# Four short TensorE transposes become plain fp32 matmuls, and the SBUF tiles are packed to 32 bytes instead of 64, in a two-layer hybrid encoder

## The chip, the cores and the metric

The kernel runs on one core of one Trainium2 chip. The metric is the device time of one execution in microseconds. Everything stays on one core, so there is no communication; the five engines (TensorE or PE, VectorE or DVE, ScalarE or ACT, GpSimd or POOL, and SyncE or SP, which only issues DMAs) work beside each other and meet through semaphores.

## The reference

Two layers over a sequence of 512 tokens of width 1024, in fp32. Each layer is

```
x = x + 0.5 * swiglu(rmsnorm(x, ffn1_norm), ...)          # D_FF = 2816
h = rmsnorm(x, mix_norm)
[q|k|v|g_out|a|b|glu|gates] = h @ w_in
q, k, v = silu(causal_conv4(q, k, v)); q, k = l2norm(q)/sqrt(128), l2norm(k)
beta = sigmoid(b);  g = -exp(a_log) * softplus(a + dt_bias)
o = gated_delta_chunked(q, k, v, g, beta)                 # 8 heads of 128
y_a = (rmsnorm(o, head_norm) * silu(g_out)) @ w_a_out
y_b = silu(rmsnorm(causal_conv31(val * sigmoid(gt)) + b, conv_norm)) @ w_b_out
x = x + (sigmoid(gate_a) * y_a + sigmoid(gate_b) * y_b) @ w_o
x = x + 0.5 * swiglu(rmsnorm(x, ffn2_norm), ...)
```

and a last `rmsnorm(x, final_norm)` follows. Inside the delta rule, with `gc` the cumulative sum of g within a chunk, the decays are `exp(gc_i - gc_j)`, a triangular system `(I + M) sol = rhs` is solved for each chunk, and the chunks of a head are then walked in order with a 128x128 state.

## The kernel before, in words

Activations lie transposed in SBUF: channels on the 128 partitions, the 512 tokens along the free axis, so a full tile is 128x512. The projections are "three-term" products: each fp32 weight tile is split into a rounded part `w_hi` and a rest `w_lo` in the fp32r format, the activations likewise (`h_hi`, `h_lo`, `act_hi`, `o_hi`, ...), and PE sums hi\*hi, hi\*lo and lo\*hi with 512 moving columns each (function `three`, line L414 for every matmul made through the helper `mm`). Weight tiles of 512 KB stream through four slots `raw`; ACT makes `w_hi`, and `w_lo` is made by DVE in the feed-forward parts and by ACT with an accumulating DMA from POOL in the mixer part.

The mixer part of a layer runs in nine sections, one PE instruction list (`PE_ORDER`) for each. In it the small fp32 products of one head's delta rule (a "round", eight per layer) are written by hand between the halves `H` of the projection of the next head, two three-term matmuls to an `H`:

```
PE_ORDER = "H H gr H H kt kk H kq H so H H x2t vt H H y0 fb H H xy0".split()
for _l in range(1, LEVELS):
    PE_ORDER += f"H H H H xt{_l - 1} y{_l} H H H xy{_l}".split()
```

PE follows this list in order, and each step waits for the semaphores of the step it needs. The steps the change touches:

- `gr` spreads the cumulative decay `gc` of the head over all partitions. It is four transposes (one for each 128-token chunk) of a single column of `hs`, read with stride 0 as a 128x128 matrix by `whole`. DVE reads the result in L1277 to form `dec`.
- `so` and `fb` belong to the head before (`tail`): `so` sums squares, DVE and POOL make the inverse root, and `fb` spreads it, again four transposes of a column. DVE uses it in L1348.
- `norm_spread` does the same for the inverse root of an RMSNorm: at the start of each feed-forward part, between the third and the fourth weight tile, and once before the mixer part of each layer.
- The last place is in the section after the ninth list, where the inverse root of the convolution's norm is spread into bank 6.

Other steps are transposes as well (`kt`, `x2t`, `vt`, `xt0` to `xt4` through the helper `turn`, L542; the entry transposes of x; the last ones of the output); these turn whole 128x128 tiles. Plain fp32 products of 128x128 tiles are made through `each`, for example `y0` to `y5` (NT with X) and `xy0` to `xy5`.

The feed-forward parts hold no such steps: PE runs through three-term products only, with DVE and ACT evicting.

All SBUF tiles are placed one behind another by the helper `sb`, each padded to a multiple of 64 bytes per partition; the counter is set back where tiles share space (`arena`, `dn_at`, `delta_at`).

Of the kernel before, what the change touches and what calls it, by code (L numbers as in the profile page):

```python
# [17 lines left out]
P = 128  # L18
# [34 lines left out]
HS_G, HS_GC, HS_NEG, HS_BETA, HS_KD, HS_GL, HS_N = 0, 1, 2, 3, 4, 5, 6  # L53
# [61 lines left out]
def trunk(nc, x, ffn1_norm, ffn1_w_gate, ffn1_w_up, ffn1_w_down, mix_norm, w_in, qkv_conv_w, a_log,  # L115
# [1 line left out]
          ffn2_w_gate, ffn2_w_up, ffn2_w_down, final_norm, consts, out):  # L117
    ds = bass.ds
    with ExitStack() as ctx:
        place = [(nc.sbuf_base + 63) // 64 * 64]  # L120

        def sb(name, shape, dt=F32):
            t = nc.alloc_sbuf_tensor_at(name, [P, *shape], dt, offset=place[0])
            place[0] += (4 * int(np.prod(shape)) + 63) // 64 * 64
            return t


        cst = sb("cst", [N_CONST, P])
        ident = cst[:, I_ID, :]
        incl = cst[:, I_INCL, :]  # L130
        ones = sb("ones", [P])
        xT = sb("xT", [KT, SEQ])
        h_hi = sb("h_hi", [KT, SEQ], F32R)
        h_lo = sb("h_lo", [KT, SEQ], F32R)
# [8 lines left out]
        nrm = sb("nrm", [4, NC])  # L143
# [37 lines left out]
        hs = sb("hs", [HS_N, NC])  # L181
        sm = sb("sm", [7, NC])
# [35 lines left out]
        bank = [ctx.enter_context(nc.psum_tensor(f"bank{i}", [P, SEQ], F32)) for i in range(8)]  # L218
# [96 lines left out]
        def whole(col):  # L315

            return col.broadcast_to([P, P])
# [94 lines left out]
        def _(pe):  # L412
            def mm(o, a, b, start=True, stop=True, **kw):
                return nc.tensor.matmul(o, a, b, start=start, stop=stop, **kw)  # L414
# [16 lines left out]
            def norm_spread(nf):  # L431
                pe.wait_ge(rs_done, nf + 1)
                for c in range(NC):
                    m = nc.tensor.transpose(bank[7][:, c * P:c * P + P], whole(nrm[:, 1, c:c + 1]), ident)
                m.then_inc(bc, 1)

            def ffn(l, w, r_f, v_f, r_d, v_d, nrm_i, nf, base_upd):
# [37 lines left out]
            for c in range(NC):  # L475
                pe.wait_ge(x_in[c], 16)
                for k in range(KT):
                    m = nc.tensor.transpose(bank[k][:, c * P:c * P + P], raw[c][:, k * P:k * P + P], ident)  # L478
                m.then_inc(xt_done, 1)

            with pe.Fori(0, DEPTH) as l:
# [3 lines left out]
                for k in range(KT):  # L485
                    m = nc.tensor.transpose(bank[k // 4][:, k % 4 * P:k % 4 * P + P], prow[:, k * P:k * P + P], ident)
# [7 lines left out]
                for k in range(KT):  # L494
                    pe.wait_ge((hlo_g, hlo_v)[k % 2], l * 4 + (k // 2 + 1))
                    for j, (wt, at) in enumerate(((wab_hi, h_hi), (wab_hi, h_lo), (wab_lo, h_hi))):
                        m = mm(bank[0][0:16, :], wt[:, k, :], at[:, k, :], start=(k == 0 and j == 0), stop=(k == KT - 1 and j == 2))
# [42 lines left out]
                def turn(o, a, name):  # L540
                    for c in range(NC):
                        m = nc.tensor.transpose(o[:, c * P:c * P + P], a[:, c * P:c * P + P], ident)  # L542
                    m.then_inc(*pe_dn.step(name))

                def stage(name, rn):

                    def ve(n, r=rn):
                        pe.wait_ge(ve_dn.sem, ve_dn.after(r, n))

                    def ac(n, r=rn):  # L550
                        pe.wait_ge(ac_dn.sem, ac_dn.after(r, n))

                    if name == "gr":
                        ve("hs")
                        for c in range(NC):
                            m = nc.tensor.transpose(bank[0][:, c * P:c * P + P], whole(hs[:, HS_GC, c:c + 1]), ident)
                        m.then_inc(*pe_dn.step(name))
                    elif name == "kt":
                        ve("kT")
                        turn(bank[1], kT, name)  # L560
                    elif name == "kk":
                        each(bank[2], kT, kT, name)
                    elif name == "kq":
                        ve("qT")
                        each(bank[3], kT, qT, name)
                    elif name == "vt":
                        ve("vT")
                        pe.wait_ge(ve_tl.sem, ve_tl.after(rn - 1, "og"))
                        turn(bank[4], va, name)
                    elif name == "x2t":  # L570
                        ve("x2T")
                        ac("eg")
                        turn(bank[0], XT, name)
                    elif name[0] == "y":
                        lv = int(name[1:])
                        ac("X2")
                        ac("kd")
                        if lv:
                            ve(f"x{lv - 1}")
                        each(bank[1], NT, X, name)  # L580
                    elif name[:2] == "xy":
                        pass
                    elif name[:2] == "xt":
                        ve("attnT")
                        ve(f"x{name[2:]}")
                        turn(bank[3], X, name)
                    elif name[:2] == "vn":
                        c = int(name[2:])
                        ac("vs")
                        if c:  # L590
                            ve(f"r{c}")
                        else:
                            ve(f"x{LEVELS - 1}")
                        mm(bank[1][:, 0:P], XT[:, c * P:c * P + P], (R[:, :] if c else vs[:, 0:P])).then_inc(*pe_dn.step(name))
                    elif name[:2] == "os":
                        c = int(name[2:])
                        t = slice(c * P, c * P + P)
                        ve(f"vn{c}")
                        pe.wait_ge(po_dn.sem, po_dn.after(rn, "qd"))
                        if c:  # L600
                            mm(bank[4][:, t], S[:, :], qd[:, t], stop=False)
                        m = mm(bank[4][:, t], VN[:, :], attn[:, t], start=(c == 0))
                        if c < NC - 1:
                            m = mm(bank[2][:, 0:P], kd[:, t], VN[:, :])
                        m.then_inc(*pe_dn.step(name))
                    elif name[0] == "p":
                        c = int(name[1:])
                        ve(f"s{c - 1}")
                        mm(bank[0][:, 0:P], kT[:, c * P:c * P + P], S[:, :]).then_inc(*pe_dn.step(name))

                def tail(name, rn):

                    if name == "so":
                        pe.wait_ge(po_tl.sem, po_tl.after(rn, "sum"))
                        pe.wait_ge(ve_tl.sem, ve_tl.after(rn - 1, "oF"))
                        for c in range(NC):
                            m = mm(bank[5][:, c:c + 1], attn[:, c * P:c * P + P], ones[:, 0:1])
                    else:
                        pe.wait_ge(po_tl.sem, po_tl.after(rn, "rs"))
                        for c in range(NC):  # L620
                            m = nc.tensor.transpose(bank[5][:, c * P:c * P + P], whole(sm[:, 5, c:c + 1]), ident)
                    m.then_inc(*pe_tl.step(name))

                def xy(lv, rn):
# [41 lines left out]
                for c in range(NC):  # L666
                    m = mm(bank[5][:, 8 + c:9 + c], csum[:, c * P:c * P + P], ones[:, 0:1])
# [9 lines left out]
                for m_ in range(PRE):  # L677
                    c = 2 * PRE + m_
                    first_unit(c)
                    for k in range(KT):  # L680
                        if m_ == 0 and k == 2:
                            pe.wait_ge(var_done, l * 4 + 3)
                            tail("so", last)
                        if m_ == 0 and k == 4:

                            pe.wait_ge(gate_done, l * (2 * PRE) + 5)
                            pe.wait_ge(rs_done, l * 4 + 3)
                            for q in range(NC):
                                m = nc.tensor.transpose(bank[6][:, q * P:q * P + P], whole(nrm[:, 1, q:q + 1]), ident)
                            m.then_inc(bc, 1)  # L690
                        if m_ == 0 and k == KT - 1:
                            tail("fb", last)
                            pe.wait_ge(ve_tl.sem, ve_tl.after(last, "olo"))
                        m = three(m_, c % SLOTS, k, o_hi, o_lo, k, k == 0, k == KT - 1)
                    m.then_inc(used, 1)
                for m_ in range(PRE):
                    c = 3 * PRE + m_
                    first_unit(c)
                    for k in range(KT):
                        if m_ == 0:  # L700
                            pe.wait_ge((clo_g, clo_v)[k % 2], l * 4 + (k // 2 + 1))
                        m = three(3 + m_, c % SLOTS, k, c_hi, c_lo, k, k == 0, k == KT - 1)
# [4 lines left out]
                with pe.Fori(0, N) as i:  # L707
                    for c in range(4):
# [7 lines left out]
                        for k in range(KT):  # L716
                            a_hi, a_lo = ((h_hi, h_lo), (h_hi, h_lo), (o_hi, o_lo), (c_hi, c_lo))[c]
                            m = three(c, c, k, a_hi, a_lo, k, k == 0, k == KT - 1)
                        m.then_inc(used, 1)

                with pe.Fori(0, 2) as i:
                    for j in range(4):
                        pe.wait_ge(lo_v, l * (V_LAYER * 4) + i * 4 + (V_O * 4 + j + 1 + SLOTS))
                        pe.wait_ge(x_upd, l * 24 + i * 4 + (16 + j - 1))
                        for k in range(KT):
                            if j == 0:
                                pe.wait_ge((mglo_g, mglo_v)[k % 2], l * 4 + (k // 2 + 1))
                            m = three(4 + j % 2, j, k, mg_hi, mg_lo, k, k == 0, k == KT - 1)
# [5 lines left out]
            for c in range(NC):  # L734
                for half in range(2):
# [3 lines left out]
                    for k in range(4):  # L739
                        m = nc.tensor.transpose(bank[n % 2][:, k * P:k * P + P], xT[:, 4 * half + k, c * P:c * P + P], ident)  # L740
# [870 lines left out]
```

## Time and profile before

| | |
|---|---|
| Runs | 2936.02, 2940.02, 2941.77 us; median 2940.02 us |
| Profiled execution | 2941.77 us, its span 2939.9 us |
| Busy share of the span | PE 97%, PE weight loads 80%, DVE 55%, ACT 38%, POOL 11% |
| Mean granted TensorE clock | 0.984 |
| DMA | 297.11 MB, mean 101 GB/s |

The span runs from the first to the last instruction of the profiled execution; 1.9 us lie around it. Times in the profile are in microseconds from the start of the span unless marked ns. "PE" is the matmul stream and "PEld" the weight loads that overlap it; the end of a matmul is modelled, so starts are the surer reading. A granted clock of 1.00 is 2.4 GHz and 0.50 is 1.2 GHz; a stretch with a change in it shows a value between. In the groups by line, the names behind `bank<-` are the operands.

### The profile page before, as it was taken

How to read it: one execution, taken by the hardware profiler on the slowest of the kernel's cores; microseconds unless marked ns; L12 is line 12 of the kernel's file. 1: busy time of each engine (PE TensorE's matmuls, PEld its weight loads, DVE VectorE, ACT ScalarE, POOL GpSimd, SP SyncE). 2: the span in 40 equal slices, each digit the busy share in tenths (PEclk: the TensorE clock that was granted, in tenths of full speed). 3: DMA queues.
4: the chain of work that ended last, by engine and by line, in shares of the span. 5: the costliest groups of instructions: out<-in, count | busy, mean ns of one | idle time of the engine just before them, and what ended most of it. 6: DMA issues, size and time to landing. Idle time of an engine off the chain costs nothing.

```text
span 2939.9 us, 40643 instructions
## 1 busy us (share of the span) xinstructions
PE 2841.8 (97%) x13920; PEld 2365.8 (80%) x13920; DVE 1623.9 (55%) x2435; ACT 1111.0 (38%) x1647; POOL 334.8 (11%) x292
## 2 busy tenths in 40 slices
PE   7999988999999999999999999799999999999999
PEld 6888867888887888888878888588888878788887
DVE  5554235888887355553255542378888853554532
ACT  4222244555553233332233222455555532323321
POOL 1000021211222010000000000221122210200001
PEclk9999989999999999999999999899999999999999
DMA  4333268666663433333333333797676745333332
GB/s 141 99 100 93 79 115 106 117 117 107 116 118 85 98 93 93 94 98 92 91 94 100 93 97 77 132 88 128 118 106 110 117 87 98 93 93 99 91 98 68
DMA packets 479234, 297.11 MB, mean 101 GB/s; under 512 B 12181, under 2 KB 462869, under 8 KB 479093
## 3 DMA queue, kind: packets, MB, share of 16 engines
q1 hardware_dynamic: 462964, 236.63, 36.6%
q0 software_dynamic: 16128, 58.73, 10.4%
q8 instruction: 72, 1.18, 0.2%
q14 instruction: 70, 0.57, 0.1%
HBM read 234.51 MB, written 2.10 MB: 80 GB/s over the span
## 4 chain that ended last, share of the span: by engine, by line
PE 84%; DMA 5%; DVE 4%; ACT 4%; issue 3%; POOL 0%; ACTq 0%; DVEq 0%; POOLq 0%; SPq 0%
PE bank L414 81%; DMA raw<-in_w_in 3%; DMA w_lo<-raw 2%; PE bank L542 2%; ACT w_hi L751 1%; ACT w_lo L753 1%; DVE cacc L1176 0%; DVE NT L1295 0%; ACT NT L886 0%; DVE XT L1300 0%; DVE w_lo L1004 0%; ACT thv L882 0%; PE bank L478 0%; DMA raw<-in_ffn_w_gate 0%; ACT dec L889 0%
## 5 line engine op out<-in xcount | busy, mean ns | idle before, releaser
L414 PE MATMUL bank<-h_hi,w_hi 128*128 128x512 f32 x2432 | 968.4, 398 | 22.9 <-DVE h_lo L1031 13.9
L414 PE MATMUL bank<-h_lo,w_hi 128*128 128x512 f32 x2432 | 969.8, 399 | 0.0
L414 PE MATMUL bank<-h_hi,w_lo 128*128 128x512 f32 x2432 | 968.2, 398 | 0.0
L751 ACT ACTIVATE w_hi<-raw 128x1024 fp32r<-128x1024 f32 x448 | 472.0, 1057 | 649.7 <-PE bank L414 604.9
L1004 DVE TENSOR_TENSOR w_lo<-raw,w_hi 128x1024 fp32r<-128x1024 f32 x336 | 413.5, 1232 | 537.9 <-ACT w_hi L751 537.0
L414 PEld LDWEIGHTS bank<-h_hi,w_hi 128*128 128x128 f32 x2432 | 461.2, 190 | 112.2 <-DVE h_lo L1031 15.4
L414 PEld LDWEIGHTS bank<-h_lo,w_hi 128*128 128x128 f32 x2432 | 461.9, 190 | 86.6
L414 PEld LDWEIGHTS bank<-h_hi,w_lo 128*128 128x128 f32 x2432 | 461.1, 190 | 85.4
L1176 DVE SCALAR_TENSOR_TENSOR cacc<-c_raw,ncol,cacc 128x512 f32<-128x512 f32 x464 | 380.7, 821 | 9.3
L414 PE MATMUL bank<-act_hi,w_hi 128*128 128x512 f32 x704 | 273.9, 389 | 0.0
L414 PE MATMUL bank<-act_lo,w_hi 128*128 128x512 f32 x704 | 273.9, 389 | 0.0
L414 PE MATMUL bank<-act_hi,w_lo 128*128 128x512 f32 x704 | 273.9, 389 | 0.0
L778 ACT ACTIVATE hf<-hf 128x512 f32<-128x512 f32 x88 | 55.6, 632 | 439.6 <-DVE hf L1046 439.6
L1495 POOL TENSOR_TENSOR ssq<-ssq,sqb 128x512 f32<-128x512 f32 x42 | 54.1, 1287 | 1440.7 <-ACT sqb L761 1440.7
L1487 POOL DMA_DIRECT2D w_lo<-raw x112 | 97.8, 907 | 595.5 <-ACT w_lo L753 575.0
L414 PEld LDWEIGHTS bank<-act_hi,w_hi 128*128 128x128 f32 x704 | 132.1, 188 | 27.7
L414 PEld LDWEIGHTS bank<-act_lo,w_hi 128*128 128x128 f32 x704 | 132.1, 188 | 27.3
L414 PEld LDWEIGHTS bank<-act_hi,w_lo 128*128 128x128 f32 x704 | 132.1, 188 | 27.3
L1048 DVE TENSOR_TENSOR sqb<-bank,ssq 128x512 f32<-128x512 f32 x88 | 60.8, 691 | 132.9 <-PE bank L414 132.7
L753 ACT ACTIVATE w_lo<-raw 128x1024 fp32r<-128x1024 f32 x112 | 118.8, 1060 | 0.0
L1046 DVE TENSOR_TENSOR hf<-bank,ssq 128x512 f32<-128x512 f32 x88 | 60.8, 691 | 102.8 <-PE bank L414 102.6
L874 ACT ACTIVATE XT<-bank 128x512 f32<-128x512 f32 x80 | 48.3, 604 | 150.9 <-PE bank L542 150.9
(238 smaller groups left out, 3127.3 us busy)
## 6 DMA issues: line engine op xcount, KB each, us to landing
raw<-in_w_in SPq DMA_DIRECT2D x128, 512.0 KB, 9.0
w_lo<-raw POOLq DMA_DIRECT2D x112, 512.0 KB, 7.3
raw<-in_ffn_w_gate SPq DMA_DIRECT2D x88, 512.0 KB, 3.8
raw<-in_ffn_w_up SPq DMA_DIRECT2D x88, 512.0 KB, 3.8
raw<-in_ffn_w_down SPq DMA_DIRECT2D x64, 512.0 KB, 3.6
raw<-in_ffn_w_down SPq DMA_DIRECT2D x32, 384.0 KB, 3.2
raw<-in_w_a_out SPq DMA_DIRECT2D x16, 512.0 KB, 4.3
raw<-in_w_b_out SPq DMA_DIRECT2D x16, 512.0 KB, 3.6
```

The source lines that it names most:

```text
L414: return nc.tensor.matmul(o, a, b, start=start, stop=stop, **kw)
L542: m = nc.tensor.transpose(o[:, c * P:c * P + P], a[:, c * P:c * P + P], ident)
L751: nc.scalar.activation(w_hi[c % SLOTS][:, :], raw[c % SLOTS][:, :], ACT.Copy).then_inc(hi_done, 1)
L753: nc.scalar.activation(w_lo[c % SLOTS][:, :], raw[c % SLOTS][:, :], ACT.Copy, scale=-1.0).then_inc(neg_done, 1)
L778: nc.scalar.activation(sg_f[c // 2][:, :], sg_f[c // 2][:, :], ACT.Silu).then_inc(silu_done, 1)
L874: nc.scalar.activation(XT[:, :], bank[3][:, :], ACT.Copy).then_inc(*ac_dn.step(f"XT{lv - 1}"))
L1004: tt(w_lo[c % SLOTS][:, :], raw[c % SLOTS][:, :], w_hi[c % SLOTS][:, :].bitcast(F32), ALU.subtract).then_inc(lo_v, 1)
L1046: tt(sg_f[f][:, :], bank[c][:, :], ssq[:, :], ALU.mult).then_inc(gs_done, 1)
L1048: tt(a_f[f][:, :], bank[c][:, :], ssq[:, :], ALU.mult).then_inc(ub_done, 1)
L1176: stt(out=dst, in0=src, scalar=ncol[:, j:j + 1], in1=cacc[:, :], op0=ALU.mult, op1=ALU.add).then_inc(taps, 1)
L1487: pool.dma_start(out=w_lo[c % SLOTS][:, :].bitcast(F32), in_=raw[c % SLOTS][:, :], accum_op=ALU.add).then_inc(lo_g[c % SLOTS], 16)
L1495: tt(ssq[:, :], ssq[:, :], sqb[m % 2][:, :], ALU.add).then_inc(sums, 1)
```

## The change

Four places that call the transpose instruction of TensorE with the identity as moving operand now call the plain matmul with the same two operands. In `gr` the operands change too: the column is `g` itself instead of its cumulative sum, and the moving matrix is the triangular matrix of ones `incl` instead of the identity, so that the product forms the cumulative sum. The waits and the other engines' instructions stay. And `sb` pads to 32 bytes instead of 64.

```diff
-        place = [(nc.sbuf_base + 63) // 64 * 64]
+        place = [(nc.sbuf_base + 31) // 32 * 32]
 
         def sb(name, shape, dt=F32):
             t = nc.alloc_sbuf_tensor_at(name, [P, *shape], dt, offset=place[0])
-            place[0] += (4 * int(np.prod(shape)) + 63) // 64 * 64
+            place[0] += (4 * int(np.prod(shape)) + 31) // 32 * 32
             return t
...
             def norm_spread(nf):
                 pe.wait_ge(rs_done, nf + 1)
                 for c in range(NC):
-                    m = nc.tensor.transpose(bank[7][:, c * P:c * P + P], whole(nrm[:, 1, c:c + 1]), ident)
+                    m = mm(bank[7][:, c * P:c * P + P], whole(nrm[:, 1, c:c + 1]), ident)
...
                     if name == "gr":
                         ve("hs")
                         for c in range(NC):
-                            m = nc.tensor.transpose(bank[0][:, c * P:c * P + P], whole(hs[:, HS_GC, c:c + 1]), ident)
+                            m = mm(bank[0][:, c * P:c * P + P], whole(hs[:, HS_G, c:c + 1]), incl)
...
                         pe.wait_ge(po_tl.sem, po_tl.after(rn, "rs"))
                         for c in range(NC):
-                            m = nc.tensor.transpose(bank[5][:, c * P:c * P + P], whole(sm[:, 5, c:c + 1]), ident)
+                            m = mm(bank[5][:, c * P:c * P + P], whole(sm[:, 5, c:c + 1]), ident)
...
                             for q in range(NC):
-                                m = nc.tensor.transpose(bank[6][:, q * P:q * P + P], whole(nrm[:, 1, q:q + 1]), ident)
+                                m = mm(bank[6][:, q * P:q * P + P], whole(nrm[:, 1, q:q + 1]), ident)
```

## Rows read from the trace of the kernel before

**Rows 1.** The page: busy time of the engines, and the chain that ended last.

```profile
PE 2841.8 (97%) x13920; PEld 2365.8 (80%) x13920; DVE 1623.9 (55%) x2435; ACT 1111.0 (38%) x1647; POOL 334.8 (11%) x292
...
PE 84%; DMA 5%; DVE 4%; ACT 4%; issue 3%; POOL 0%; ACTq 0%; DVEq 0%; POOLq 0%; SPq 0%
```

**Rows 2.** Groups on PE, shapes apart: count, then busy us, mean ns, idle before.

```profile
L414 PE MATMUL bank<-X,NT 128*128 128x128 f32 x768 | 102.5, 277 | 0.0
...
L556 PE MATMUL bank<-cst,hs 128*128 128x128 f32 x64 | 10.9, 297 | 9.3 <-DVE hs L1267 9.3
...
L621 PE MATMUL bank<-cst,sm 128*128 128x128 f32 x64 | 9.6, 272 | 0.0
...
L434 PE MATMUL bank<-cst,nrm 128*128 128x128 f32 x24 | 4.6, 326 | 6.1 <-POOL nrm L1499 6.1
```

**Rows 3.** Timeline of PE in a round: start us, us, instruction, count.

```profile
703.92 0.60 PE L542 MATMUL bank<-cst,X 128*128 128x128 f32 x4
704.35 1.06 PE L414 MATMUL bank<-X,NT 128*128 128x128 f32 x8
705.16 0.48 PE L414 MATMUL bank<-h_lo,w_hi 128*128 128x512 f32 x1
705.48 0.39 PE L414 MATMUL bank<-h_hi,w_lo 128*128 128x512 f32 x1
705.71 0.40 PE L414 MATMUL bank<-h_hi,w_hi 128*128 128x512 f32 x1
```

**Rows 4.** Timeline of PE at the start of the first feed-forward part.

```profile
43.86 0.60 PE L434 MATMUL bank<-cst,nrm 128*128 128x128 f32 x4
...
44.53 0.39 PE L414 MATMUL bank<-h_lo,w_hi 128*128 128x512 f32 x1
```

**Rows 5.** Timeline of the start of a steady round; in brackets idle before, and releaser.

```profile
627.39 0.60 PE L556 MATMUL bank<-cst,hs 128*128 128x128 f32 x4
...
628.02 1.13 DVE L1277 TENSOR_SCALAR dec<-bank,hs 128x128 f32<-128x128 f32 x4
...
631.37 0.17 DVE L1283 TENSOR_SCALAR sm<-ksum 128x4 f32<-128x4 f32 x1 [0.96 <-ACT NT L886]
...
633.49 0.40 PE L414 MATMUL bank<-h_hi,w_hi 128*128 128x512 f32 x1
...
634.59 0.65 PE L542 MATMUL bank<-cst,XT 128*128 128x128 f32 x4 [0.70 <-DVE XT L1300]
```

**Rows 6.** Chain that ended last, same round: start us, us, what.

```profile
611.82 14.37 PE bank L414 x76
...
626.29 0.05 ACT hf L849
...
637.70 0.44 PE bank L621 x4
```

**Rows 7.** Waits of PE, whole span: total us, times, longest.

```profile
PE bank L542 <- DVE XT L1300: 10.7, 14, 1.1
...
PE bank L414 <- DMA w_lo<-raw: 8.5, 3, 3.1
```

**Rows 8.** Busy time by stretch: the columns end with granted clock, DMA share, GB/s.

```profile
512.70:516.20 3.50, 3.44 (x10) 2.84 (x11) 0.54 (x3) 2.96 (x4) 0.00 (x0) 0.52 0.80 129
```

**Rows 9.** Chain that ended last, before and in the first round of layer 0.

```profile
394.99 1.13 PE bank L434 x4
...
451.20 0.95 PE bank L556 x4
```

**Rows 10.** Chain that ended last, last round of layer 0 and the section after.

```profile
896.37 0.73 DVE XT L1261
...
918.35 0.44 PE bank L689 x4
...
920.87 0.45 PE bank L621 x4
```

**Rows 11.** One line of DVE: duration ns min/median/max.

```profile
L1176 DVE SCALAR_TENSOR_TENSOR cacc<-c_raw,ncol,cacc x464: 726/752/2097, 470.5 to 2358.6; 128x512 f32<-128x512 f32 x155
```

## The prediction

> **What bounds the kernel now.** I read the page first: PE is busy 97% of the span, and the chain of work that ended last runs over PE for 84% of it [rows 1]. So what PE must do longer is paid unless it falls into one of PE's few waits. Next I read the groups of PE with the shapes kept apart, to see what a transpose and a plain fp32 product of the same size are on this engine [rows 2]; then the timeline of PE, for what each costs in the stream [rows 3, 4]; then the timeline and the chain of one steady round, the waits of PE, and the places outside the steady rounds, to see which of the changed steps has a wait behind it that swallows it [rows 5 to 10].
>
> The reader is to see two things. First, the code asks for 4 x 6 x 16 = 384 products `NT,X`, and the trace has 768 matmuls of that form; for `gr` it asks for 4 x 16 = 64 transposes, and the trace has 64 [rows 2]. A plain fp32 product is two weight loads with two matmuls, a transpose is one. Second, in a round PE waits in one place, for DVE L1300 before `x2t`, about 0.7 us [rows 5]; in all 14 such waits with 10.7 us [rows 7], in 14 of the 16 rounds.
>
> **The cost of one group of four.** The step of the stream is 0.23 us for a three-term matmul [rows 3]. From the start of four transposes to the second matmul behind them are 44.53 - 43.86 = 0.67 us [rows 4]; less one step of 0.23, four transposes take 0.44. From the start of four transposes, with eight plain matmuls (four products) behind them, to the second matmul behind those are 705.48 - 703.92 = 1.56 us [rows 3]; less 0.23 and 0.44, four plain products take 0.89. So each group that changes costs PE 0.89 - 0.44 = 0.45 us more at full clock. At the low clock, the same columns take twice the time: a group of four at 394.99 stands with 1.13 us where it has 0.60 at full clock [rows 4, 9], so I take 0.9 us there.
>
> The Trainium skill, TensorE: Matmul & The Clock Gate, section Terms, calls the transpose mode four times faster for FP32. By that a plain group would take 1.76 us instead of 0.89 and the change would cost 1.32 a group instead of 0.45. The trace does not agree: it shows 0.89 for four products, twice the transposes, and I go by the trace.
>
> **The change part by part.** The groups: `gr` 64/4 = 16, `fb` 64/4 = 16, `norm_spread` 24/4 = 6 [rows 2], and two in bank 6 (one per layer): 40.
>
> - *`fb`, 12 in the rounds.* It stands between `y0` and the halves that follow, behind the wait at `x2t`, and it is on the chain (L621 at 637.70) [rows 6]. Nothing waits between it and the end of the round; the next round's wait does not shrink either, since the work that it waits for starts with ACT L849 at 626.29, right behind PE's last three-term matmuls of the section before [rows 6]: it moves with PE. 12 x 0.45 = 5.4 us. The rounds are 16; the first of each layer has no `fb` before it, and the last of each layer ends otherwise (next).
> - *`fb`, 2 in the last round of each layer.* That round has all 31 taps of the convolution on DVE, and the chain goes over DVE before the first `vn` (XT L1261 at 896.37) [rows 10]. PE is ahead of DVE there: 0. Without that cover, 0.9.
> - *`fb` for the last head, 2, and bank 6, 2.* Both are on the chain at 918.35 and 920.87, with DVE waiting [rows 10]: 4 x 0.45 = 1.8.
> - *`norm_spread` in the feed-forward parts, 4.* PE runs without a break there [rows 4]: 4 x 0.45 = 1.8.
> - *`norm_spread` ahead of the mixer part, 2.* On the chain, at the low clock [rows 9]: 2 x 0.9 = 1.8.
> - *`gr`, 12 in rounds with the wait.* PE reaches `x2t` 0.45 later and finds it not later: its last matmul before starts at 633.49, so it could go on at 633.72, and XT comes at 634.59; 0.87 us of slack for 0.45. But `gr` also feeds DVE: L1277 would start at 628.47 instead of 628.02 and DVE be 0.45 later until L1283, where it sits idle 0.96 us for ACT's squares [rows 5]. Both covers are wider than the delay: 0. What is late next without them is `x2t` itself, 0.45 each.
> - *`gr`, 2 in the first round of each layer.* PE starts it out of a wait for `hs`, at the low clock, and everything of the round hangs on it (L556 at 451.20 is on the chain) [rows 9]: 2 x 0.9 = 1.8. In layer 0 one of the three waits for the `w_lo` transfer [rows 7] comes before the next round and may swallow it.
> - *`gr`, 2 in the rounds without the wait at `x2t`.* These are the second rounds; that of layer 0 is at the low clock (granted 0.52 from 512.7) [rows 8]. 0.9 + 0.45 = 1.35.
> - *`incl` for the identity, `g` for `gc`.* Same shape, another 128x128 tile of the same constant array; 0. `gc` is still made, since DVE needs it.
> - *32 bytes instead of 64.* Tiles from `hf` on move down by 32 to 256 bytes. Some, among them `act_hi`, `o_hi`, `c_hi` and `mg_hi`, come to lie at 32 bytes past a multiple of 64. No big DMA target moves. DVE's taps read `c_raw` at every multiple of 4 bytes, and of 464 the shortest takes 726 and the median 752 ns [rows 11] (the longest are held up by something else), so the start address makes no difference above some 3% on DVE. PE's moving operand at such an address is in no row. I take 0; the bound above is in the rivals.
>
> Sum: 5.4 + 1.8 + 1.8 + 1.8 + 1.8 + 1.35 = 13.95, so 14 us. Against the profiled execution, 2941.77 us, that is 2955.8; it lies 1.75 us above the median of the runs, 2940.02, so the forecast for a median is 2954 us, slower by 0.48%.
>
> **The rivals.**
>
> - *All 40 groups are paid.* Something in the 12 rounds moves with `gr` after all, say ACT's squares behind `kt`, which is also 0.45 later. Then 12 + 2 more groups: 14 x 0.45 = 6.3, in sum 20.3 us: 2960. Against it are the 0.96 us of idle DVE and 0.87 us of PE [rows 5]; for it, that the chain to `x2t` runs through ACT right behind. 12 in 100.
> - *Not slower: a round's pace is not PE's.* If DVE or the weight transfers set when a round ends, whatever PE gets in one vanishes; it decides from the point where they need 0.45 us more than PE in each round. Left are 8 groups outside the rounds at full clock and the two ahead of the mixer parts at the low one: 8 x 0.45 + 2 x 0.9 = 5.4 us: 2945.4, +0.18%. For it are three waits for a transfer with 8.5 us; against it, that they are three in the whole span [rows 7] and that the steady round's chain is PE's [rows 6]. 10 in 100.
> - *The address costs on PE.* If a moving row off a multiple of 64 bytes cost one cycle of 2.4 GHz for each 64 bytes, that would be 32 cycles, 13 ns, for each of 3264 matmuls over `act`, `o`, `c` and `mg` (by the code's loops 2112 + 3 x 384): 43 us more, 2997 in all. No row speaks for it; the nearest, DVE's taps, speaks against. 5 in 100.
> - *The plain product costs more than in `each`* (four times a transpose): the 20 open groups at 1.32, 26; the low clock ones at 2.6, 14; `gr` past its slack of 0.87 twelve times, 5: 45 us, 2985. 2 in 100.
> - *Faster through the clock.* The granted clock is 0.984 in the mean; if plain matmuls in place of transposes brought it up sooner after each of PE's waits, the gain would be half of the low stretch they cut. To end faster by 0.2% it would have to give 20 us, cutting 40 us of low clock. The stretches at the low clock next to changed groups are about 3 to 4 us each [rows 8] and six in number, 24 us in all. 2 in 100.
>
> The Trainium skill (same page, Part 4: PE-mode transpose) says that transposes do not count as busy for the clock. If so, the first rounds' `gr` and the two spreads would bring the clock up to 0.9 us sooner, worth up to 0.45 each, and the sum would be 12 instead of 14.
>
> **How the numbers follow.** A measurement of this kernel tells about 0.2%, 5.9 us, from no change (its three runs lie within 5.75 us). The forecast's own chance is 66 in 100, with 3 left for what I have not seen. The range goes from the rival with 5.4 us, 2945, to a little past the rival with all groups paid, 2962; it leaves out the address, the dear product and the faster clock. Slower by over 0.2%: 87 in 100; within 0.2%: 11; faster: 2.
>
> **What would show it.** In the profile after, the forms at `gr`, `fb` and the spreads should be counted twice, 128 for each 64, and PE have 160 more matmuls. From `y0` to the second matmul behind `fb` should be 0.45 us more. The wait at `x2t` should shrink from 0.7 to about 0.3 us, with `x2t` no later behind ACT L849. The step of the stream should stay 0.23 us over `act_hi` as over `h_hi`. I am wrong if rounds keep their length, if `x2t` moves with `gr`, or if that step changes.

## The result and the profile after

The changed kernel takes 2970.5 us in the median of four runs (2968.7 to 2972.0), the kernel before 2940.9 in four runs on the same chip (2936.0 to 2945.4). The medians lie 29.6 us apart. The ratio is 1.0095, 95% interval 1.0082 to 1.0108, which is 28 us; the record holds ten runs of the changed kernel in all, from 2965.5 to 2972.0, with a mean of 2968.7. So it is slower by 28 us, where 14 were forecast and 2962 was the upper end of the range.

The page after, first the busy time of each engine and then the chain that ended last:

```profile
PE 2879.1 (97%) x14080; PEld 2388.2 (80%) x14080; DVE 1622.7 (55%) x2435; ACT 1110.2 (37%) x1647; POOL 334.9 (11%) x292
...
PE 87%; DVE 4%; ACT 3%; DMA 3%; issue 3%; POOL 0%; ACTq 0%; DVEq 0%; POOLq 0%; SPq 0%
```

PE has 160 matmuls more, as foreseen, and still bounds the kernel; its share of the chain rose [rows 1]. The groups of PE after, shapes apart (count, busy us, mean ns of one, idle before):

```profile
L414 PE MATMUL bank<-h_lo,w_hi 128*128 128x512 f32 x2432 | 968.0, 398 | 0.0
...
L414 PE MATMUL bank<-act_hi,w_hi 128*128 128x512 f32 x704 | 279.1, 396 | 0.0
L414 PE MATMUL bank<-act_lo,w_hi 128*128 128x512 f32 x704 | 279.1, 396 | 0.0
L414 PE MATMUL bank<-act_hi,w_lo 128*128 128x512 f32 x704 | 279.1, 396 | 0.0
L414 PE MATMUL bank<-X,NT 128*128 128x128 f32 x768 | 102.2, 276 | 0.0
...
L414 PE MATMUL bank<-cst,hs 128*128 128x128 f32 x128 | 18.9, 295 | 11.1 <-DVE hs L1267 11.1
L414 PE MATMUL bank<-cst,sm 128*128 128x128 f32 x128 | 16.9, 275 | 0.0
L414 PE MATMUL bank<-cst,nrm 128*128 128x128 f32 x64 | 10.5, 316 | 5.5 <-POOL nrm L1499 5.5
```

The forms of `gr` and `fb` stand twice as often as before [rows 2]. The other thing to see is the products over `act`, which no edit to a matmul touched. In the kernel before they and those over `h` stood so:

```profile
L414 PE MATMUL bank<-h_lo,w_hi 128*128 128x512 f32 x2432 | 969.8, 399 | 0.0
...
L414 PE MATMUL bank<-act_hi,w_hi 128*128 128x512 f32 x704 | 273.9, 389 | 0.0
```

Over `act` they are no longer at 389 ns but at 396, while over `h` hardly anything moved. Matmuls overlap, so their mean duration isn't what the stream pays; that is the distance from one start to the next. The timeline of PE after, in the down projection of the first feed-forward part:

```profile
299.94 0.40 PE L414 MATMUL bank<-act_hi,w_hi 128*128 128x512 f32 x1
300.18 0.39 PE L414 MATMUL bank<-act_lo,w_hi 128*128 128x512 f32 x1
300.41 0.40 PE L414 MATMUL bank<-act_hi,w_lo 128*128 128x512 f32 x1
300.64 0.40 PE L414 MATMUL bank<-act_hi,w_hi 128*128 128x512 f32 x1
300.88 0.39 PE L414 MATMUL bank<-act_lo,w_hi 128*128 128x512 f32 x1
```

and in the same projection of the kernel before:

```profile
298.65 0.39 PE L414 MATMUL bank<-act_hi,w_hi 128*128 128x512 f32 x1
...
299.56 0.39 PE L414 MATMUL bank<-act_lo,w_hi 128*128 128x512 f32 x1
```

Four steps take 0.94 us after, 0.235 each, and 0.91 before. Rounded to 0.01 us that is hardly to be told from 0.23, so from here on I give the *step*: the mean distance of successive starts in the trace over all three-term matmuls of one operand that follow each other within 260 ns. Over `act` it went from 226.7 to 234.3 ns, over `o` from 227.3 to 234.0, over `mg` from 226.9 to 234.2; over `h` (227.8 and 227.5) and `c` (231.7 and 231.3) it stayed. Times their counts, 2112 x 7.6 = 16.1 us for `act` and 768 x 7.1 = 5.4 us for `o` and `mg`: 21.5 us that the sum of the forecast had at 0.

The same, by stretches of the two profiled executions (spans 2939.9 and 2967.5 us, so +27.6). The marks are POOL L1499, which ends each norm's inverse root, and DVE L1267, which starts each round:

| stretch | change, us |
|---|---|
| four feed-forward parts, from one L1499 to the next | +4.44, +4.42, +4.44, +4.44 |
| rounds 3 to 8 of each layer (5 distances of L1267) | +1.82, +1.98 |
| from the inverse root to the third round | +2.77, -1.03 |
| eighth round to the inverse root behind it | -0.27, -0.23 |
| output projections and `norm` up to the feed-forward part | +1.40, +4.48 |
| start and end of the kernel | -0.19, -0.91 |

Each feed-forward part holds 528 matmuls over `act` (4.0 us) and one group of `norm_spread` (0.45). Together that is 4.45 us, where 4.42 to 4.44 were measured.

The steady round after, in the timeline of its engines (in brackets the idle time before, and its releaser):

```profile
633.66 0.60 ACT L849 ACTIVATE hf<-bank 128x512 f32<-128x512 f32 x1 [3.11 <-PE bank L414]
...
634.76 1.05 PE L414 MATMUL bank<-cst,hs 128*128 128x128 f32 x8
...
635.85 1.13 DVE L1277 TENSOR_SCALAR dec<-bank,hs 128x128 f32<-128x128 f32 x4 [0.50 <-PE bank L414]
...
638.73 0.17 DVE L1283 TENSOR_SCALAR sm<-ksum 128x4 f32<-128x4 f32 x1 [0.50 <-ACT NT L886]
...
641.96 0.65 PE L542 MATMUL bank<-cst,XT 128*128 128x128 f32 x4 [0.24 <-DVE XT L1300]
...
644.91 1.06 PE L414 MATMUL bank<-cst,sm 128*128 128x128 f32 x8
645.72 0.47 PE L414 MATMUL bank<-h_hi,w_lo 128*128 128x512 f32 x1
646.03 0.39 PE L414 MATMUL bank<-h_hi,w_hi 128*128 128x512 f32 x1
```

Against [rows 5, 6]: from ACT L849 to `x2t` are 8.30 us before (626.29 to 634.59) and 8.30 after (633.66 to 641.96). The idle time ahead of `x2t` went from 0.70 to 0.24 us, that ahead of DVE L1283 from 0.96 to 0.50. From the start of `fb` to the second matmul behind it are 1.12 us, 0.89 without one step.

### The profile page after: what moved, and what is told of

It reads as the page before. It is cut to its first block, busy times and chain, and to the rows that moved or that the text cites. A ratio compares the mean times of both kernels' runs of the same rounds, so it can differ in the third digit from the quotient of the medians.

```text
span 2967.5 us, 40963 instructions
## 1 busy us (share of the span) xinstructions
PE 2879.1 (97%) x14080; PEld 2388.2 (80%) x14080; DVE 1622.7 (55%) x2435; ACT 1110.2 (37%) x1647; POOL 334.9 (11%) x292
## 4 chain that ended last, share of the span: by engine, by line
PE 87%; DVE 4%; ACT 3%; DMA 3%; issue 3%; POOL 0%; ACTq 0%; DVEq 0%; POOLq 0%; SPq 0%
PE bank L414 85%; PE bank L542 2%; DMA raw<-in_w_in 2%; ACT w_hi L751 1%; DMA w_lo<-raw 1%; ACT w_lo L753 1%; ACT NT L886 1%; DVE NT L1295 1%; DVE cacc L1176 0%; DVE XT L1300 0%; ACT dec L889 0%; ACT qd L890 0%; PE bank L478 0%; DVE w_lo L1004 0%; DMA raw<-in_ffn_w_gate 0%
```

## The experiments

Two parts are to be told apart, the matmuls and the padding. Of the second, I wanted to know what about the addresses matters.

**`e1_pad32`**: the padding alone.

```diff
-        place = [(nc.sbuf_base + 63) // 64 * 64]
+        place = [(nc.sbuf_base + 31) // 32 * 32]
...
-            place[0] += (4 * int(np.prod(shape)) + 63) // 64 * 64
+            place[0] += (4 * int(np.prod(shape)) + 31) // 32 * 32
```

> The kernel before with the 32-byte padding alone; all transposes stay. Theory A (the address of PE's moving operand costs): the step of the three-term stream is 234 ns over act, o and mg, as in the changed kernel, where it is 227 before, and 228 over h; with 7.4 ns for 2112 matmuls over act and 7 for 768 over o and mg this gives 21 us, 2961 us. Rival B (the slower step comes with the plain matmuls, not with the addresses): step 227 everywhere, 2940 us.

**`e2_matmuls`**: the four edits to the matmuls alone, padding as before.

> The four matmul edits alone, padding 64 bytes as before. Theory A: step 227 ns over act; the time is the sum of the prediction for the matmuls, or somewhat less, since six of the steady rounds of layer 0 and 1 are only 0.4 us longer each: 7 to 14 us, 2947 to 2954 us. Rival B: step 234 ns over act, about 2965 us or more.

Times against the kernel before on the same chip (2938.1 us, 27 runs): the padding alone 2954.8 (6 runs), ratio 1.0057 [1.0033, 1.0082]; the matmuls alone 2948.5 (10 runs), 1.0038 [1.0024, 1.0052]. Together 0.95%, the whole. The same group on PE in the first and then in the second:

```profile
L414 PE MATMUL bank<-act_hi,w_hi 128*128 128x512 f32 x704 | 279.1, 396 | 0.0
```

```profile
L414 PE MATMUL bank<-act_hi,w_hi 128*128 128x512 f32 x704 | 273.9, 389 | 0.0
```

The steps of the first are those of the changed kernel (`act` 234.3, `o` 234.0, `mg` 234.3), those of the second those of before (226.7, 227.0, 226.9). The steps make 21.5 us. The median of the padding alone grew by 16.7 us, with 10 to 24 by the interval. The span of its profiled execution grew by 21.8, but that execution is the slowest of its six (2963.6 us), so the close match with 21.5 is partly luck. The rounds of the first take 56.37 us as before (56.40), those of the second 56.87.

**`e3_gr`** and **`e4_fb`**: one line each.

```diff
-                            m = nc.tensor.transpose(bank[0][:, c * P:c * P + P], whole(hs[:, HS_GC, c:c + 1]), ident)
+                            m = mm(bank[0][:, c * P:c * P + P], whole(hs[:, HS_G, c:c + 1]), incl)
```

> Only gr as plain matmuls, padding 64 bytes. If gr is hidden behind the wait before x2t, a steady round stays 56.40 us from hs to hs and the wait of PE shrinks from 0.70 to about 0.3 us; in all 0 to 3 us more, 2940 to 2943 us. Rival: each round 0.45 us longer, 7 us in all, 2947 us.

```diff
-                            m = nc.tensor.transpose(bank[5][:, c * P:c * P + P], whole(sm[:, 5, c:c + 1]), ident)
+                            m = mm(bank[5][:, c * P:c * P + P], whole(sm[:, 5, c:c + 1]), ident)
```

> Only fb as plain matmuls, padding 64 bytes. If fb is paid in each steady round, that round is 56.8 to 56.9 us from hs to hs instead of 56.40, and the whole 6 to 7 us longer, 2947 us. Rival (something else sets the pace of a round): a round stays 56.40 us and the time 2941 us or less.

`gr` alone: 2938.0 us (10 runs), 0.999 [0.9974, 1.0007], steady rounds of 56.40 to 56.43. For all of `gr` this interval ends at 2 us more. `fb` alone: 2942.8 (10 runs), 1.0024 [1.001, 1.0039], which is 7 us [3, 11], though the medians lie only 4.7 apart; its steady rounds take 56.86, which is 0.46 more. The steady round of `gr` alone, timeline:

```profile
629.84 0.60 ACT L849 ACTIVATE hf<-bank 128x512 f32<-128x512 f32 x1 [3.17 <-PE bank L414]
...
630.93 1.05 PE L414 MATMUL bank<-cst,hs 128*128 128x128 f32 x8
...
638.14 0.65 PE L542 MATMUL bank<-cst,XT 128*128 128x128 f32 x4 [0.25 <-DVE XT L1300]
```

Again 8.30 us from L849 to `x2t`; the whole of the longer `gr` went into the wait, 0.70 to 0.25. `fb` has no such wait behind it in a steady round and is paid. What the edits do outside the steady rounds can't be told from single profiles: from the inverse root to the third round of a layer, the two layers of before take 176.2 and 175.1 us, those of `gr` alone 179.4 and 174.5, those of `fb` alone 171.7 and 171.7, those of all four edits 180.4 and 176.7. They differ by more than the 4.95 us that the forecast put there, and `fb` alone is shorter than before.

**`e5_arena32`, `e6_arena64`, `e7_arena96`**: the kernel before, with a gap of 32, 64 or 96 bytes ahead of `arena`. `act`, `o`, `mg` and all behind them move up by so much; the weight slots and `h` stay.

```diff
+        place[0] += 32
         arena = place[0]
```

> The kernel before with 32 bytes left free ahead of the arena, so that every tile from x_sq on starts 32 bytes higher and nothing else moves against anything. If the start of PE's moving operand past a multiple of 64 bytes is the cause: step 234 ns over act, o and mg, 227 over h, about 21 us more. If another of the moved tiles of the change was the cause (hf, small ones): step 227.

> As the run with 32 bytes, but with 64, which puts the arena's tiles at 64 past a multiple of 128 and c_lo, which was at 64 before, at a multiple of 128. If only the distance from a multiple of 64 bytes counts: step 227 ns over act, o and mg, the time as before. If the distance from a multiple of 128 counts: 234 or more, near 241 if it grows with the distance, 21 to 42 us more.

> As the run with 32 bytes, but with 96. Counting from multiples of 64 bytes: step 234 ns over act as at 32, 21 us more. Counting from 128 and growing with the distance: near 248 ns. Counting from 128 as a yes or no: 234 ns at 32, 64 and 96 alike.

**`e8_clo128`**: only `c_lo` (with `cth` behind it), which in the kernel before starts 64 bytes past a multiple of 128, is moved up by 64 and starts on one.

```diff
-        place[0] = delta_at
+        place[0] = delta_at + 64
         c_lo = sb("c_lo", [KT, SEQ], F32R)
```

> The kernel before with c_lo alone moved up by 64 bytes, from 64 past a multiple of 128 to a multiple of 128. The step over c was 230 to 233 ns in every run so far where act and o were at 227. If c_lo's place at 64 of 128 is the reason, the step over c falls to 227 and the time by some 2 us; if the reason is another (what runs beside it), it stays 231.

One run each, against one of before on the same chip (2943.7 us): 2952.7, 2939.6, 2949.1 and 2940.4. The steps, in ns:

| | `h` | `act` | `o` | `mg` | `c` |
|---|---|---|---|---|---|
| before | 227.8 | 226.7 | 227.3 | 226.9 | 231.7 |
| gap of 32 | 227.8 | 233.3 | 233.3 | 233.3 | 232.4 |
| gap of 64 | 227.7 | 228.9 | 229.5 | 229.0 | 231.4 |
| gap of 96 | 227.9 | 233.4 | 233.7 | 233.3 | 233.2 |
| `c_lo` up by 64 | 227.8 | 226.7 | 227.2 | 226.8 | 229.8 |

The gaps of 32 and 96 were expected to cost some 21 us, by the steps they cost about 19, and the single runs show 9 and 5. The steps are paid all the same: in the profile with the gap of 32 the four feed-forward parts together are 13.5 us longer than before, for 2112 x 6.6 = 13.9 by the step. But the stretches from the inverse root to the third round are 5.2 us shorter there (10 us with the gap of 96), and these are the ones that vary from kernel to kernel. Single times are therefore no measure of a gap; the steps are.

It isn't a cost that grows with the distance from a multiple of 128: 64 bytes cost a third of what 32 and 96 cost, and its 2112 x 2.2 = 4.6 us are below what single runs tell. The expectation for 64 had 227 or at least 234 ns and missed with both. So did that for `c_lo`: the step over `c` neither stayed at 231.7 nor fell to 227, it went to 229.8. Nor is the cost the same for the three terms. The groups with a gap of 96:

```profile
L415 PE MATMUL bank<-act_hi,w_lo 128*128 128x512 f32 x704 | 280.9, 399 | 0.0
L415 PE MATMUL bank<-act_lo,w_hi 128*128 128x512 f32 x704 | 277.4, 394 | 0.0
L415 PE MATMUL bank<-act_hi,w_hi 128*128 128x512 f32 x704 | 276.0, 392 | 0.0
```

and with a gap of 32, where all three are alike:

```profile
L415 PE MATMUL bank<-act_hi,w_hi 128*128 128x512 f32 x704 | 278.1, 395 | 0.0
L415 PE MATMUL bank<-act_hi,w_lo 128*128 128x512 f32 x704 | 278.1, 395 | 0.0
L415 PE MATMUL bank<-act_lo,w_hi 128*128 128x512 f32 x704 | 278.1, 395 | 0.0
```

That the cost of a matmul depends on which weights it goes with or which are loaded beside it points away from the moving operand's own start. In the kernel before, `w_hi`, `w_lo`, `h`, `act`, `o`, `mg` and `c_hi` all start at multiples of 128 bytes, and at multiples of 256 from each other. So a start of its own and a distance to the weights can't be told apart there. The next three do that.

**`e9_all32`**: all tiles up by 32 bytes, distances as before.

```diff
-        place = [(nc.sbuf_base + 63) // 64 * 64]
+        place = [(nc.sbuf_base + 63) // 64 * 64 + 32]
```

> The kernel before with all of SBUF's tiles 32 bytes higher, weights and activations alike. Theory A (what counts is where the moving operand itself starts): step 233 to 234 ns over act, o and mg, and now over h too, 10560 matmuls at some 6.7 ns, 71 us more. Rival C (what counts is the distance between the moving operand's start and that of the weights that are loaded beside it): 227 everywhere, the time as before.

**`e10_w32`**: the weight slots `w_hi` and `w_lo` up by 32. `h` lies ahead of them and stays; what lies behind them moves up by 128 in all, so that `act` keeps its start modulo 128 and is 96 bytes further from the weights.

```diff
+        place[0] += 32
         w_hi = [sb(f"w_hi{s}", [UNIT], F32R) for s in range(SLOTS)]
         w_lo = [sb(f"w_lo{s}", [UNIT], F32R) for s in range(SLOTS)]
+        place[0] += 96
         row_at = place[0]
```

> The kernel before with w_hi and w_lo alone at 32 bytes past a multiple of 64, the activations where they were. Theory A: 227 ns, the time as before. Rival C: 233 to 234 everywhere, 70 us more. A third outcome, that weight loads have the same cost of their own: 227 too as long as a weight load of 190 ns stays under the step.

**`e11_acthi32`**: `act_hi` alone up by 32, with 96 more ahead of `act_lo`.

```diff
+        place[0] += 32
         act_hi = sb("act_hi", [FT, SEQ], F32R)
+        place[0] += 96
         act_lo = sb("act_lo", [FT, SEQ], F32R)
```

> The kernel before with act_hi alone at 32 bytes past a multiple of 128; act_lo, o, mg and c as before. If each matmul pays for its own moving operand, two of three over act take some 6.7 ns more: 2112 x 2/3 x 6.7 = 9.4 us. If the step is held up by another thing in the feed-forward parts, all three or none.

With 2940.6 us for the kernel before (13 runs, 2932.6 to 2943.8), they take 2936.6, 2984.7 and 2950.2 in one run each. Groups of the first, with everything off by 32:

```profile
L414 PE MATMUL bank<-h_lo,w_hi 128*128 128x512 f32 x2432 | 967.9, 398 | 0.0
...
L414 PE MATMUL bank<-act_hi,w_hi 128*128 128x512 f32 x704 | 273.9, 389 | 0.0
```

Groups of the second, with only the weights off:

```profile
L416 PE MATMUL bank<-h_lo,w_hi 128*128 128x512 f32 x2432 | 979.2, 403 | 0.0
...
L416 PE MATMUL bank<-act_hi,w_lo 128*128 128x512 f32 x704 | 280.9, 399 | 0.0
L416 PE MATMUL bank<-act_lo,w_hi 128*128 128x512 f32 x704 | 277.4, 394 | 0.0
L416 PE MATMUL bank<-act_hi,w_hi 128*128 128x512 f32 x704 | 276.0, 392 | 0.0
```

Groups of the third, with only `act_hi` off:

```profile
L416 PE MATMUL bank<-act_hi,w_hi 128*128 128x512 f32 x704 | 278.8, 396 | 0.0
L416 PE MATMUL bank<-act_hi,w_lo 128*128 128x512 f32 x704 | 276.0, 392 | 0.0
L416 PE MATMUL bank<-act_lo,w_hi 128*128 128x512 f32 x704 | 276.0, 392 | 0.0
```

A start off a multiple of 64 costs nothing if the weights have it too: every step of the first is that of before. Moving the weights alone makes the products over `h` dear, which no other run touched (233.2 ns), and gives those over `act` exactly the three values of the gap of 96, which is the distance that they now have. It is thus the distance between the start of the moving operand and that of the weights which counts, and the theories of a start of its own, of the operand or of the weights, are out.

A rival is left: ACT and DVE write weights and activations into SBUF all the while, and it could be their accesses that PE now meets. The trace of the padding alone speaks against it. Of its steps over `act`, the 432 that lie to nine tenths or more under instructions of ACT take 234.2 ns, the 1456 in which ACT does nothing 234.3; with DVE the two means are 234.2 and 234.3. The longer step comes whether or not these engines work, so their accesses aren't needed for it. What in the chip makes it stays open.

The second was expected to take 70 us more and takes 44 (43 by the span of its profile). They lie nearly all in the four feed-forward parts, +10.1, +10.8, +10.1 and +10.7. There the step over `h` went from 226.8 to 233.3; in a steady round it was 231.3 already in the kernel before and went to 232.6, and the round grew only from 56.40 to some 56.5. Why a round's products over `h` step at 231 at all stays open.

The third was expected at 9.4 us more, with two of the three terms dearer, and takes 9.6; the time agrees by luck. All three terms became dearer: 235.0 for `act_hi,w_hi`, 229.2 for `act_hi,w_lo`, 229.2 for `act_lo,w_hi`. The first two have the same moving operand and weights of the same phase and differ by 6 ns, so what stands next to a matmul in the stream counts too. The test is also less clean than its expectation says, since `act_lo` was moved as well, by 128 bytes. How the cost divides over the terms isn't explained by these runs.

**`e12_pad32_aligned`**: padding to 32 as in the change, transposes as before, and the two starts rounded up again.

```diff
+        place[0] = (place[0] + 127) // 128 * 128
         arena = place[0]
...
+        place[0] = (place[0] + 127) // 128 * 128
         delta_at = place[0]
```

> The kernel before (with its transposes) and padding to 32 bytes, but the two starts arena and delta_at rounded up to 128. If the moved small tiles and the raw tiles at 32 past a multiple of 64 cost ACT, DVE, POOL and the DMAs nothing, the time is that of before, or 1 to 2 us less by c_lo at a multiple of 128: 2936 to 2941 us. If the padding costs elsewhere than in PE's stream, some part of the 17 us of the padding alone is left.

2938.4 us (10 runs), ratio 0.9999 [0.9987, 1.0011]. The steps are 226.7 over `act`, 227.3 over `o`, 226.8 over `mg`, and 226.9 over `c`, which is less than before. The tiles `hf`, `k_raw`, `v_raw`, `c_raw`, `cacc` and some small ones still start at 32 past a multiple of 64, and that costs the engines that use them no more than some 5 us in all (3 by the interval, and 2 that `c` gives back). So the padding's cost goes away with the two starts; the steps say that it lay on PE. As the two starts put back the large tiles for every engine at once, this run alone doesn't show that ACT, DVE or POOL pay nothing for them.

## Why the prediction was wrong, point by point

- *32 bytes instead of 64, taken as 0*: **this is the step that failed**, with 21.5 us by the steps and 17 [10, 24] by the runs of the padding alone. The prediction saw that `act_hi`, `o_hi` and `mg_hi` change their phase and that no row shows PE reading such an address, and then took the value from DVE's row [rows 11]. That row is about another engine; it bounds nothing on PE. With the term open, its bound belonged into the range, which left it out as one of the rivals.
- *The rival on the addresses on PE* named the place and was given 5 in 100. Its size was 13 ns for each matmul and 43 us; measured are 7.1 to 7.6 ns on `act`, `o` and `mg`, and none more on `c`. Its rule, a start off a multiple of 64, is wrong: `e9_all32` has it everywhere and pays nothing.
- A trace of before held a hint that was not read. The groups over `c` and over `mg`, in the kernel before:

```profile
L414 PE MATMUL bank<-c_lo,w_hi 128*128 128x512 f32 x128 | 51.1, 399 | 0.0
...
L414 PE MATMUL bank<-mg_lo,w_hi 128*128 128x512 f32 x128 | 49.8, 389 | 0.0
```

  Same line, shape and count, and 10 ns apart. `c_lo` was the one large moving operand that did not start at a multiple of 128, and its step was 231.7 against 226.9. That row would have put a price of some 5 ns on a shifted operand, 2880 x 5 = 14 us for `act`, `o` and `mg`, as one end of the range. That it would have been so near is luck: the distance there was 64, which costs `act` only 2.2 ns, and 32 costs 7.6. The DVE row was also read a little too well: from 726 to 752 ns are 3.6%, not 3.
- *The cost of one group of four, 0.45 us*: right. Measured from the start of the group to the second matmul behind it, less a step, are 0.440 us for four transposes and 0.897 for four products, so 0.46. The Trainium skill, TensorE: Matmul & The Clock Gate, section Terms, calls the transpose mode four times faster for FP32; the trace after shows twice here, and by the four times the rounds of `fb` alone would have grown by 1.32 us, not by 0.46.
- *`fb` in the rounds, 5.4 us*: right where it can be seen, which is 10 of the 12: 0.42 to 0.48 more in each steady round of `e4_fb` and `e2_matmuls`, apart from one of 58.64 us in `e4_fb` (`e1_pad32`, which has the transposes, shows one of 58.15 at the same place). The other two lie in the stretch that varies.
- *`fb` in the last round, 0*: right; from the eighth round to the inverse root behind it the time is 0.2 to 0.3 us shorter, not longer.
- *`gr` in the steady rounds, 0*: right, and by the covers named: the wait at `x2t` and the idle time ahead of DVE L1283 both shrank by 0.46 us, and `x2t` kept its 8.30 us behind ACT L849. The rival with all 40 groups paid is out.
- *`norm_spread` in the feed-forward parts, 1.8*: right within what is left of +4.44 when the 528 matmuls over `act` are taken off. In `e2_matmuls`, where `act` isn't slower, these parts grew by 0.41, -0.29, 0.42 and 0.74 us, 1.3 in sum.
- *`gr` in the first two rounds and `norm_spread` ahead of the mixer part, 4.95*: not to be seen in single profiles, since that stretch varies by more from kernel to kernel. The part for `gr`, 1.8 + 1.35 = 3.15 us, was too large: the ten runs of `gr` alone end at 2 us more. Without it the sum would be 10.8, and the four matmul edits cost 11 us [7, 15]; but 14, and the 12 that the prediction gives for a clock that rises sooner, lie in that interval too.
- *A round's pace is not PE's*: out; `fb` alone lengthens each steady round by its own cost. *The plain product costs more*: out by the 0.46. *Faster through the clock*: the granted clock is 0.984 before and after.
- In the changed kernel the steady round is 56.77 to 56.84 us, a little under the 56.87 of the matmul edits alone, though `h` and the weights lie the same. `NT`, `X` and `XT` do lie at multiples of 128 there and 64 past them before. That this is the reason was not tried.

## What to carry to other kernels

Where PE is the bound and streams moving operands past freshly loaded weights, the large moving tiles and the weight slots should keep the same start modulo 256 bytes per partition. At an odd multiple of 128 the steps in these runs were 229 to 230 ns, not 227. A distance of 32 or 96 cost 3% of each matmul of 512 columns, 64 a third of that, and an allocator's padding can change this without a line of the compute being touched. A longer step of PE is free as far as the wait behind it reaches (here 0.46 us of 0.70), and is paid in full where none follows before the engine's next work that others wait for. An open cost without a row on its own engine keeps both ends in the range; a look at groups of one line and shape that differ in nothing but the tile would have shown the price.

## What was not expected of the hardware

- The distance in SBUF between the moving operand and the weights prices an fp32r matmul of 128x512: 226.7 ns from start to start at a multiple of 256, 228.9 at 64, and, counted modulo 128, 233.3 to 234.3 at 32 and 233.4 at 96; the absolute start doesn't (226.7 with all tiles up by 32).
- 128 bytes are probably not the whole period. At 32 past a multiple of 128 the step is 233.3 where the distance is 32 past a multiple of 256 (`e5_arena32`) and 234.3 where it is 160 past one (the changed kernel and `e1_pad32`). And `h` in `e10_w32` is 224 past a multiple of 256 away from the weights, with all three terms at 233 ns, while `act` in the same run is 96 past one, with terms from 231 to 238. In `e8_clo128` the start of `c_lo` is a multiple of 128 but not of 256 away from that of the weights, and the step over `c` is 229.8; in `e12_pad32_aligned` it is a multiple of 256 away, and the step is 226.9. The gap in `e11_acthi32` put `act_lo` 128 bytes off too, with 229.2. Other things differ in each of these pairs, and no run was made to test it.
- The kernel before paid for this already on `c`: 384 x 4.8 = 1.8 us, which `e12_pad32_aligned` takes back, too little for the runs to tell.
- An effect of these starts on the other engines or the transfers wasn't seen, but the runs could not have told one below some 5 us.
- Distances below 32 bytes weren't tried, and what in the chip makes the cost stays open.
